# A hybrid streaming-encoder layer on one core: first rows taken by halves, a second plain feature tile, the down projection's first pieces split inside gate and up, attention's loads on another queue

## The chip, the cores and the metric

The kernel runs on one core of a Trainium2 chip. The metric is device time in microseconds (us) of one execution; the median of three runs is given. One further execution was taken by the hardware profiler, and all rows come from it.

## What is computed

One layer on x of 1024 rows (frames) by 1024 features, all float32:

```
x = x + 1/2 * swiglu(rms_norm(x), gate, up, down)       # FFN 1, d_ff = 2816
P = rms_norm(x) @ w_in                                   # 1024 x 3584
A = chunked band attention, 8 heads x 64, q and k RMS-normed, 9 chunks of 64 keys, relative bias
B = HGRN2 gated recurrence, 4 heads x 128, chunkwise, per-head RMS norm, swish gate
x = x + concat(A, B) @ w_out
x = x + 1/2 * swiglu(rms_norm(x), gate2, up2, down2)     # FFN 2
```

## The kernel before, in words

The instructions of each engine are written out by hand in program order; each engine is a strict queue, and semaphores order them against each other. There is no planner: where a line stands in its engine's list decides when it can run. Every matrix product is done three times in a reduced-precision float type (`three`, L636 to L638): high part times high part, high times low, low times high. So each operand is first split: ScalarE (ACT) copies it to its high part, VectorE (DVE) subtracts to get the low part.

**Stages, in order.** FFN 1: rows are normalised, transposed (features on partitions, `hThi`, `hTlo`) and multiplied. Gate and up go over 22 feature tiles of 128; each tile is 7 block products (Strassen-like, `gate_up`, which need sums t1, t2, t34 of the transposed rows, `hXhi`/`hXlo`, and sums of weights), only tile 0 is done plainly in 8 products (`plain`). A product is 12 matmuls of 128x512. The order at the start is the hand list `START` (15 products), the order in which weights are split is `WEIGHTS` (11, then 7 a tile), in a ring of 8 half places (`weight`). After product n both ACT and DVE prepare the weight that `PREPARED_AFTER` or `prepared_after` names, 7 products ahead. Down is 77 pieces (7 products x 11 pairs) in a ring of 4 (`piece_hi`, `piece_lo`, L1156 and L1568), of 12 matmuls each; its first piece is split when all 155 products are in. Then come the input projection (7 groups of 8 blocks, each of the last four with an HGRN head's matmuls hooked in), attention, the output projection in two column halves, and FFN 2 with the same code (F = 1).

**Start.** SyncE (SP) issues rows 0 to 3 of x (tiles of 128), gate and up of tile 0, rows 4 to 7, gate and up of tile 1. For each row tile ACT squares (L1047), GpSimd (POOL) takes the root (L1895, L1898), DVE normalises 1024 features (L1411), PE makes 8 transposes (L670), ACT copies the result back into `xs` (`keep_turned`, L1068) and from there to the high part (L1072), DVE makes the low part (L1425). The first product waits for four row tiles with all features. Product (1, 3) waits for `u2_ready`, which DVE gives at L1532 behind the weights of products to come.

**Attention.** Per pair of heads (4 pairs) there are 12 units; PE makes scores (L892), DVE adds the bias and takes the maximum (L1814), ACT exponentiates (L1335), PE turns (L905), DVE or ACT copies back (L1823, L1343), PE multiplies by values (L925). The first scores wait for `ro_ready`, the scaling of the last HGRN head's read-out (DVE L1763), whose banks they overwrite. POOL issues all loads: q and k (`load_qk`, L2036), bias (`load_bias`, L2040), v (`load_v`, L2044); it masks two corners of each bias tile after it has landed (`mask_bias`, L2052, L2053), scales q and k by their roots (`qk_rms`, L2060, L2063), and does the last head's gating (`finish`, L1998 to L2003) in between, all in one queue. Before exponentials of pair p come to an end ACT squares q and k of pair p + 1 (`square_qk`, L1285).

**Output projection.** SP issues w_out's pieces, then gate and up of FFN 2's tiles 0 and 1 (L501), then for each row tile the store of x (L620); the normalise of FFN 2 writes in place and waits for that store. PE turns tile t - 1 after row t of the second half. DVE's and ACT's first weights of FFN 2 come after all eight row tiles.

**End.** `take` (L1594) adds each of the last product's four banks once all 12 matmuls of the last piece are in; each is then stored.

Of the kernel before, what the change touches and what calls it, by code (L numbers as in the profile page):

```python
# [52 lines left out]

def slot(m):

    return (m + 1) % RING


def loads(m):
# [24 lines left out]

PLAIN_WEIGHT = (0, 1, 2, 3, 2, 3, 0, 1)
# [5 lines left out]
START = [(0, 0), (0, 1), (1, 0), (0, 2), (0, 3), (1, 2), (0, 4), (0, 5), (0, 6), (0, 7),  # L91
         (1, 4), (1, 1), (1, 3), (1, 5), (1, 6)]
PRODUCTS = START + [(e, i) for e in range(2, FT) for i in range(NPROD)]
WEIGHTS = [(0, 0), (0, 1), (1, 0), (0, 2), (0, 3), (1, 2), (1, 4), (1, 1), (1, 3), (1, 5), (1, 6)]\
    + [(e, i) for e in range(2, FT) for i in range(NPROD)]
# [5 lines left out]
PREPARED_AFTER = {8: [8], 9: [9, 10], 10: [11, 12], 11: [13], 12: [14, 15], 13: [16], 14: [17]}  # L101
# [6 lines left out]
def weight_no(e, i):  # L108
    return WEIGHTS.index((e, PLAIN_WEIGHT[i] if e == 0 else i))


def last_use(w):

    e, i = WEIGHTS[w]
    return seq(e, max(q for q in range(8) if PLAIN_WEIGHT[q] == i)) if e == 0 else seq(e, i)


def prepared_after(n):
    if n <= 14:
        return PREPARED_AFTER.get(n, [])  # L120
    return [n + 3] if n + 3 < NW else []
# [9 lines left out]
RAW_RING = 8  # L131
EVACS = NPROD * 4

# [50 lines left out]
def turn_bank(R, t):  # L184

    if R == R_FFN1:
        return (0, 2, 4, 6, 2, 6, 2, 6)[t]
# [4 lines left out]
    return 2 * (t % 2)  # L192

# [12 lines left out]
def build(nc, x, ffn1_norm_g, ffn1_w_gate, ffn1_w_up, ffn1_w_down, mix_norm_g, w_in, attn_q_norm_g,  # L206
# [3 lines left out]
    with ExitStack() as ctx:  # L210
# [50 lines left out]
        with ExitStack() as c:  # L261
            hThi = keep("hThi", [P, KT, T], F32R, c)
            hTlo = keep("hTlo", [P, KT, T], F32R, c)
            with ExitStack() as c2:
                hXhi = keep("hXhi", [P, 12, HALF], F32R, c2)
                hXlo = keep("hXlo", [P, 12, HALF], F32R, c2)
                gu_q = keep("gu_q", [P, HALF], where=c2)
# [40 lines left out]

        relrow = aT[0:AH, 0:N_REL]
# [6 lines left out]
        def weight(buf, w, F):  # L316

            at = (w + 2 * F) % PLACES
            return buf[:, at // 2, at % 2 * HALF:(at % 2 + 1) * HALF]

        def raw_weight(w):
# [3 lines left out]
            if e == 0:  # L325
# [38 lines left out]
        hT_ready = sem("hT_ready")  # L364
        z_copied = sem("z_copied")
# [70 lines left out]
        bias_loaded = sem("bias_loaded")  # L436
        bias_masked = sem("bias_masked")
# [31 lines left out]
        def score_bank(v):  # L469

            return 2 * ((v + 1) % 2)
# [6 lines left out]
        def _(sp):  # L478
            def piece(m, adv, src, shape):
# [5 lines left out]
                dst = raw[:, slot(m), :]  # L485
                if shape:
                    dst = dst.rearrange("p (k c) -> p k c", k=shape)
                sp.dma_start(dst, src).then_inc(raw_loaded[slot(m)], 16)

            def gate_up(F, e, w_gate, w_up):  # L490

                if e >= 2:
                    sp.wait_ge(w_ready, NW * F + (weight_no(e - 2, S4) if e > 2 else weight_no(0, 3)) + 1)
# [119 lines left out]
            for h in range(2):  # L613
# [1506 lines left out]
```

## Time and profile before

| | us |
|---|---|
| median of 3 runs (1974.49 to 1977.51) | 1974.71 |
| the profiled execution's own time | 1979.15 |
| its span, first to last instruction | 1977.6 |
| TensorE (PE) busy in it | 1897.7 |
| VectorE (DVE) busy | 1116.0 |
| ScalarE (ACT) busy | 676.9 |
| GpSimd (POOL) busy | 440.3 |

The profiled execution took 1.55 us more than its span, and 4.4 us more than the median. A view of the waits lists for each engine what ended its idle times; the chain of waits follows the last instruction back in time; the timeline gives each instruction with its start, its length and, in brackets, the idle time before it with its releaser. Matmul records overlap, so the pace of a row of matmuls is the distance of their starts. The granted TensorE clock is 1.00 at 2.4 GHz and about half in stretches at 1.2 GHz.

### The profile page before, as it was taken

To read this page: it belongs to the slowest core of one execution; us is meant where nothing else is said; L and a number is where in the kernel's file an instruction comes from. 1 tells how busy PE (TensorE), PEld (TensorE's weight loads), DVE (VectorE), ACT (ScalarE), POOL (GpSimd) and SP (SyncE) were. 2 spreads that over 40 slices of the span, in tenths; PEclk is the share of its full clock that TensorE was granted. 3 is DMA by queue.
4 is the path that set the end of the run, shared out by engine and by line. 5 is a ranking of instruction groups with operands and counts; after the bars stand their busy time and mean duration, and the time that the engine had idled before them with its cause. 6 is when DMAs were issued, how large, how long until landed. Compare 5 with 4: busy or idle time off the path is not lost.

```text
span 1977.6 us, 24542 instructions
## 1 busy us (share of the span) xinstructions
PE 1897.7 (96%) x9296; PEld 1570.5 (79%) x9296; DVE 1116.0 (56%) x1503; ACT 676.9 (34%) x1023; POOL 440.3 (22%) x350
## 2 busy tenths in 40 slices
PE   6899999999999999999998789989999999999998
PEld 5788888887888888888887567777888888878887
DVE  6866666665555630244545664348666666655564
ACT  7333333323333432211122563244333223323332
POOL 3322422431111100011223420001422422321030
PEclk9999999999999999999998999999999999999999
DMA  5454444537755343321342410114354444468663
GB/s 163 144 183 148 159 169 146 175 135 283 247 193 195 107 155 112 117 96 64 127 142 90 144 57 1 64 64 149 139 179 146 165 162 152 149 226 284 216 195 132
DMA packets 209004, 295.50 MB, mean 149 GB/s; under 512 B 14512, under 2 KB 104760, under 8 KB 208896
## 3 DMA queue, kind: packets, MB, share of 16 engines
q1 hardware_dynamic: 193184, 253.28, 37.5%
q0 software_dynamic: 7360, 25.51, 4.0%
q10 hardware_dynamic: 8352, 15.27, 2.1%
q8 instruction: 68, 1.11, 0.2%
q14 instruction: 40, 0.33, 0.1%
HBM read 205.37 MB, written 91.25 MB: 150 GB/s over the span
## 4 chain that ended last, share of the span: by engine, by line
PE 89%; DVE 5%; issue 2%; ACT 2%; DMA 1%; POOL 1%; DVEq 0%; SPq 0%; ACTq 0%; POOLq 0%
PE ps L636 27%; PE ps L638 27%; PE ps L637 27%; PE ps L809 2%; PE ps L670 1%; PE ps L905 1%; PE ps L892 1%; PE ps L925 1%; DVE wlo L1494 1%; DVE hXlo L1465 0%; DVE xs L1447 0%; DMA tok_scratch<-y 0%; DVE hTlo L1425 0%; DMA xs<-x 0%; PE ps L800 0%
## 5 line engine op out<-in xcount | busy, mean ns | idle before, releaser
L636 PE MATMUL ps<-hThi,whi 128*128 128x512 f32 x864 | 338.7, 392 | 11.9 <-DVE wlo L1494 6.4
L637 PE MATMUL ps<-hTlo,whi 128*128 128x512 f32 x864 | 337.6, 391 | 0.0
L638 PE MATMUL ps<-hThi,wlo 128*128 128x512 f32 x864 | 337.5, 391 | 0.0
L636 PE MATMUL ps<-whi 128*128 128x512 f32 x616 | 241.7, 392 | 9.2 <-DVE wlo L1568 9.2
L638 PE MATMUL ps<-whi,wlo 128*128 128x512 f32 x616 | 241.1, 391 | 0.0
L637 PE MATMUL ps<-wlo,whi 128*128 128x512 f32 x616 | 241.1, 391 | 0.0
L636 PE MATMUL ps<-hXhi,whi 128*128 128x512 f32 x504 | 197.9, 393 | 8.8 <-DVE wlo L1494 8.8
L636 PEld LDWEIGHTS ps<-hThi,whi 128*128 128x128 f32 x864 | 163.1, 189 | 46.0 <-DVE wlo L1494 6.6
L637 PE MATMUL ps<-hXlo,whi 128*128 128x512 f32 x504 | 197.3, 391 | 0.0
L638 PE MATMUL ps<-hXhi,wlo 128*128 128x512 f32 x504 | 197.3, 391 | 0.0
L638 PEld LDWEIGHTS ps<-hThi,wlo 128*128 128x128 f32 x864 | 163.0, 189 | 34.1
L637 PEld LDWEIGHTS ps<-hTlo,whi 128*128 128x128 f32 x864 | 163.2, 189 | 33.6
L1494 DVE TENSOR_TENSOR wlo<-raw,whi 128x512 fp32r<-128x512 f32 x176 | 128.4, 731 | 103.5 <-ACT whi L1103 103.5
L636 PE MATMUL ps<-whi,hThi 128*128 128x512 f32 x448 | 180.3, 403 | 1.1 <-DVE hTlo L1425 1.1
L638 PE MATMUL ps<-whi,hTlo 128*128 128x512 f32 x448 | 175.5, 392 | 0.0
L637 PE MATMUL ps<-wlo,hThi 128*128 128x512 f32 x448 | 174.7, 390 | 0.0
L1568 DVE TENSOR_TENSOR wlo<-raw,whi 128x1024 fp32r<-128x1024 f32 x80 | 113.6, 1426 | 83.1 <-ACT whi L1156 83.1
L1922 POOL TENSOR_TENSOR hidS<-hid 128x512 f32<-128x512 f32 x22 | 36.0, 1635 | 523.8 <-DVE hid L1562 523.8
L1103 ACT ACTIVATE whi<-raw 128x512 fp32r<-128x512 f32 x176 | 110.1, 627 | 123.3 <-PE ps L638 122.0
L636 PEld LDWEIGHTS ps<-whi 128*128 128x128 f32 x616 | 116.6, 189 | 34.3 <-DVE wlo L1568 10.0
L1568 DVE TENSOR_TENSOR wlo<-rawx,whi 128x1024 fp32r<-128x1024 f32 x74 | 93.9, 1269 | 81.4 <-ACT whi L1156 81.4
L638 PEld LDWEIGHTS ps<-whi,wlo 128*128 128x128 f32 x616 | 116.5, 189 | 24.5
(186 smaller groups left out, 2959.7 us busy)
## 6 DMA issues: line engine op xcount, KB each, us to landing
hid_scratch<-hid SPq DMA_DIRECT2D x132, 256.0 KB, 2.6
raw<-ffn_w_gate SPq DMA_DIRECT2D x44, 512.0 KB, 3.7
raw<-ffn_w_up SPq DMA_DIRECT2D x44, 512.0 KB, 4.9
wdb<-ffn_w_down SPq DMA_DIRECT2D x44, 512.0 KB, 4.1
wd_scratch<-wdb SPq DMA_DIRECT2D x88, 256.0 KB, 4.5
raw<-hid_scratch SPq DMA_DIRECT2D x80, 256.0 KB, 2.7
rawx<-hid_scratch SPq DMA_DIRECT2D x74, 256.0 KB, 2.7
raw<-w_in SPq DMA_DIRECT2D x28, 512.0 KB, 5.2
```

The lines of the kernel that those rows point to most:

```text
L636: pe.matmul(dst, ahi, bhi, start=first, stop=False, skip_group_check=onto)
L637: pe.matmul(dst, ahi, blo, start=False, stop=False, skip_group_check=onto)
L638: return pe.matmul(dst, alo, bhi, start=False, stop=last, skip_group_check=onto)
L670: mm = pe.transpose(ps[:, c0 + k * P:c0 + (k + 1) * P], src[:, k * P:(k + 1) * P], ident[:, :])
L809: mm = pe.matmul(ps[:, b * HALF + c * 64:b * HALF + (c + 1) * 64], hK[:, c * P:(c + 1) * P], q[:, c, :, 1, :], start=True, stop=True)
L892: last[hd] = pe.matmul(ps[:, b + c:b + c + m], qT[rows, p % 2, t * P:(t + 1) * P], kT[rows, p % 2, lo + c - c0:lo + c - c0 + m], start=Tru ...
L905: mm = pe.transpose(ps[:, 4 * HALF + c * P:4 * HALF + (c + 1) * P], Pr[:, v % SLOTS, c * P:(c + 1) * P], ident[:, :])
L925: mm = pe.matmul(ps[rows, b:b + P], vin[:, p % 2, t - n + 1 + c, rows], PT[:, (2 * w + hd) % SLOTS, c0 + c * P:c0 + (c + 1) * P], start=(c ...
L1103: act.activation(weight(whi, w, F), raw_weight(w), ACT.Copy).then_inc(w_hi_ready, 1)
L1494: dve.tensor_tensor(weight(wlo, w, F), raw_weight(w), weight(whi, w, F).bitcast(F32), ALU.subtract).then_inc(w_ready, 1)
L1568: dve.tensor_tensor(wlo[:, s, :], raw_piece(n), whi[:, s, :].bitcast(F32), ALU.subtract)\
L1922: pool.tensor_tensor(hidS[:, :], a11, a21, ALU.subtract).then_inc(hid_sums, 1)
```

## The change

In five places. **Start of FFN 1:** rows 0 to 3 are normalised, transposed and split by halves of 512 features (`early_norm`, `early_turn`, `early_hi_part`, `early_lo_part`; `early_keep` copies back afterwards from the bank), and the first product waits for the first halves alone; gate and up of tile 1 are loaded ahead of rows 4 to 7. **Both FFNs:** tile 1 is plain too (`NPLAIN` = 2, 8 products in place of 7, 156 in all), so the sums t1, t2, t34 are first needed at tile 2. **Down:** pieces 0 to 2 are split after products 1, 3 and 4 of the last tile; the ring places are shifted so that they fall in places that are free by then. **Attention:** SP issues the q, k, bias and v loads, bias and v of pairs 0 and 1 together, and the second half of w_out after them; the two masked corners are written once into the bias scratch in HBM by two DMAs of POOL; the first scores no longer wait for the read-out (head 1's go to banks 6 and 7), the read-out follows DVE's first two score passes. **Output projection and end:** gate and up of FFN 2 are issued after the stores of row tiles 2 and 4; FFN 2's first two weights are split before the last row tile; the last piece signals after each of its four banks.

```diff
+def raw_slot(m):
+    return (m + 1) % RING
 def slot(m):
-    return (m + 1) % RING
+    return (m + 3) % RING
...
+NPLAIN = 2
-START = [(0, 0), (0, 1), (1, 0), (0, 2), (0, 3), (1, 2), (0, 4), (0, 5), (0, 6), (0, 7),
-         (1, 4), (1, 1), (1, 3), (1, 5), (1, 6)]
+START = [(0, 0), (0, 1), (1, 0), (1, 1), (0, 2), (0, 3), (1, 2), (1, 3),
+         (0, 4), (0, 5), (1, 4), (1, 5), (0, 6), (0, 7), (1, 6), (1, 7)]
-PREPARED_AFTER = {8: [8], 9: [9, 10], 10: [11, 12], 11: [13], 12: [14, 15], 13: [16], 14: [17]}
+PREPARED_AFTER = {12: [8], 13: [9], 14: [10], 15: [11, 12], 16: [13, 14, 15]}
...
+PIECE_AFTER = [(FT - 1, 1), (FT - 1, 3), (FT - 1, 4)]
+def piece_slot(F, n):
+    return (n + 2 + 3 * F) % RING
+def early_bank(t):
+    return (2, 3, 6, 7)[t]
 def score_bank(v):
-            return 2 * ((v + 1) % 2)
+            return 6 if v == 1 else 2 * ((v + 1) % 2)
 # SyncE
             gate_up(0, 0, ffn1_w_gate, ffn1_w_up)
+            gate_up(0, 1, ffn1_w_gate, ffn1_w_up)
             for t in range(4, TT):
                 sp.dma_start(xs[:, t, :], x[0, t * P:(t + 1) * P, :]).then_inc(x_loaded[t], 16)
-            gate_up(0, 1, ffn1_w_gate, ffn1_w_up)
...
-            for e in range(2):
-                gate_up(1, e, ffn2_w_gate, ffn2_w_up)
+            out_pieces(0)
+            stored(6)
+            sp.wait_ge(y_ready, 2 * TT)
+            sp.wait_ge(turned, 2 * TT)
+            load_qk(0)
+            sp.wait_ge(bias_stored, 48)
+            sp.wait_ge(proj_done, PROJ_OUTS)
+            load_bias(0)
+            load_bias(1)
+            sp.wait_ge(qk_turned, 4)
+            load_qk(1)
+            stored(7)
+            load_v(0)
+            load_v(1)
+            out_pieces(1)
+            for p in range(2, PAIRS):
+                sp.wait_ge(qk_turned, 4 * p)
+                load_qk(p)
+                sp.wait_ge(unit_out, NU * (p - 1))
+                load_bias(p)
+                load_v(p)
             for t in range(TT):
                 sp.wait_ge(x_added, TT + t + 1)
                 sp.dma_start(x_d[t * P:(t + 1) * P, :], xs[:, t, :]).then_inc(x_saved[t], 16)
+                if t in (2, 4):
+                    gate_up(1, t // 2 - 1, ffn2_w_gate, ffn2_w_up)
 # TensorE
-                mm.then_inc(piece_done, 1)
+                    if t == 3 or F and n == NPIECE - 1:
+                        mm.then_inc(piece_done, 1)
...
             for t in range(4):
+                early_turn(t, 0)
+            products(0, 0, 1)
+            early_turn(0, 1)
+            early_turn(1, 1)
+            products(0, 1, 2)
+            early_turn(2, 1)
+            early_turn(3, 1)
+            for t in range(4, TT):
+                products(0, t - 2, t - 1)
                 turn_tile(R_FFN1, t)
+            products(0, 6, SEQ)
...
                 if w:
                     pe.wait_ge(unit_max, 2 * w)
                 else:
+                    pe.wait_ge(proj_evac, PROJ_OUTS)
+                if w == 1:
                     pe.wait_ge(ro_ready, HH + 1)
 # ScalarE, start
+            for t in range(3):
+                square(R_FFN1, t)
+            early_hi_part(0, 0)
+            square(R_FFN1, 3)
+            weight_hi(0, 0)
+            for t in range(1, 4):
+                early_hi_part(t, 0)
+            weight_hi(0, 1)
             for t in range(4):
+                early_keep(t, 0)
+            weight_hi(0, 2)
+            early_hi_part(0, 1)
+            early_hi_part(1, 1)
+            weight_hi(0, 3)
+            early_keep(0, 1)
+            early_keep(1, 1)
+            early_hi_part(2, 1)
+            early_hi_part(3, 1)
+            weight_hi(0, 4)
+            early_keep(2, 1)
+            early_keep(3, 1)
+            weight_hi(0, 5)
+            for t in range(4, TT):
                 square(R_FFN1, t)
 # ScalarE, last group of the projection: take_qk(0, 4) now ahead of the last split
+                    if q == 2 and square_at:
+                        act.wait_ge(proj_done, PROJ_OUTS)
+                        act.wait_ge(qk_gain_ready, 1)
+                        take_qk(0, 4)
 # ScalarE, FFN 2
-            for t in range(TT):
+            for t in range(TT - 1):
                 square(R_FFN2, t)
                 if t >= 2:
                     keep_turned(R_FFN2, t - 2)
+            weight_hi(1, 0)
+            weight_hi(1, 1)
+            square(R_FFN2, TT - 1)
+            keep_turned(R_FFN2, TT - 3)
 # ScalarE and VectorE, both FFNs (piece_hi on one, piece_lo on the other)
+                for n in range(12, SEQ):
+                    after_product(F, n)
+                    if PRODUCTS[n] in PIECE_AFTER:
+                        piece_hi(F, PIECE_AFTER.index(PRODUCTS[n]))
 # VectorE
+                if not prepare:
+                    read_out(j)
...
+            dve.wait_ge(bias_stored, 48)
...
+                if v == 1:
+                    read_out(HH - 1)
 # GpSimd
+            pool.memset(masked, MASKED).then_inc(mhalf_set, 1)
...
+            pool.dma_start(bias_d[:, CHUNK:P, 0:CHUNK].rearrange("h t s -> t h s"), corner)\
+                .then_inc(bias_stored, 16)
+            pool.dma_start(bias_d[:, 0:CHUNK, BAND - CHUNK:BAND].rearrange("h t s -> t h s"), corner)\
+                .then_inc(bias_stored, 16)
...
-            load_qk(0)
-            load_bias(0)
-            load_v(0)
-            mask_bias(0)
             finish(HH - 1)
             for p in range(1, PAIRS):
-                pool.wait_ge(qk_turned, 4 * p)
-                load_qk(p)
-                load_bias(p)
-                load_v(p)
-                mask_bias(p)
-                if p == 1:
+                if p == 2:
                     pool.wait_ge(ro_stored, 16 * HH)
```

## Rows read from the trace of the kernel before

**Rows 1.** The page: the span and the busy time of each engine.
```profile
span 1977.6 us, 24542 instructions
PE 1897.7 (96%) x9296; PEld 1570.5 (79%) x9296; DVE 1116.0 (56%) x1503; ACT 676.9 (34%) x1023; POOL 440.3 (22%) x350
```

**Rows 2.** Timeline, start of FFN 1, PE and DVE: start, length, what, [idle before].
```profile
14.48 1.29 DVE L1411 SCALAR_TENSOR_TENSOR xs<-xs,rstd,gain 128x1024 f32<-128x1024 f32 x1 [0.72 <-POOL rstd L1898]
22.40 0.77 PE L636 MATMUL ps<-hThi,whi 128*128 128x512 f32 x1 [5.48 <-issue]
27.62 1.91 PE L670 MATMUL ps<-ident,xs 128*128 128x128 f32 x16
...
67.77 0.77 PE L636 MATMUL ps<-hXhi,whi 128*128 128x512 f32 x1 [6.52 <-DVE wlo L1494]
```

**Rows 3.** Timeline of the same stretch, DVE further on.
```profile
45.75 2.49 DVE L1441 TENSOR_TENSOR xs<-xs 128x512 f32<-128x512 f32 x4
...
66.99 0.68 DVE L1532 TENSOR_TENSOR gu_u<-ps,gu_s 128x512 f32<-128x512 f32 x1
```

**Rows 4.** Chain of waits, start: one square of 128x1024 and its sum's read.
```profile
9.61 1.16 ACT junk L1047 x2
```

**Rows 5.** Timeline from gate and up to down, FFN 1: PE and SP's queue.
```profile
451.78 0.39 PE L638 MATMUL ps<-hThi,wlo 128*128 128x512 f32 x1
...
458.58 0.39 PE L638 MATMUL ps<-hThi,wlo 128*128 128x512 f32 x1
463.57 0.80 PE L636 MATMUL ps<-whi 128*128 128x512 f32 x1 [4.60 <-DVE wlo L1568]
...
467.96 0.39 PE L637 MATMUL ps<-wlo,whi 128*128 128x512 f32 x1
...
445.43 0.44 SPq L553 DMA_DIRECT2D raw<-ffn_w_down  x1
```

**Rows 6.** Timeline from projection to attention: ACT, PE, POOL.
```profile
1074.12 1.11 ACT L1302 ACTIVATE kT<-ps,qkg 128x1024 f32<-128x1024 f32 x1
...
1077.93 2.51 PE L892 MATMUL ps<-kT,qT 64*128 64x512 f32 x8 [4.89 <-DVE kS L1763]
1082.29 2.50 PE L892 MATMUL ps<-kT,qT 64*128 64x512 f32 x8 [1.85 <-DVE nmax L1814]
...
1094.71 1.33 PE L905 MATMUL ps<-ident,Pr 128*128 128x128 f32 x5 [5.74 <-ACT Pr L1335]
...
1087.10 0.89 POOL L2036 DMA_DIRECT2D y<-tok_scratch  x1
...
1092.79 1.06 ACT L1285 ACTIVATE junk<-y 128x1024 f32<-128x1024 f32 x1 [9.53 <-DMA y<-tok_scratch]
```

**Rows 7.** Timeline inside pair 1: POOL right after its masks, and PE.
```profile
1129.66 0.20 POOL L2060 TENSOR_SCALAR rsq<-ssq 128x16 f32<-128x16 f32 x1
...
1135.76 0.74 PE L905 MATMUL ps<-ident,Pr 128*128 128x128 f32 x5 [2.44 <-DVE PT L1823]
```

**Rows 8.** Timeline, output projection: SP's queue, DVE, PE.
```profile
1273.34 48.80 SPq L620 DMA_DIRECT2D x_scratch<-xs  x8
1279.38 1.28 DVE L1411 SCALAR_TENSOR_TENSOR xs<-xs,rstd,gain 128x1024 f32<-128x1024 f32 x1 [6.07 <-DMA x_scratch<-xs]
1280.72 1.97 PE L670 MATMUL ps<-ident,xs 128*128 128x128 f32 x8 [2.70 <-DVE xs L1411]
```

**Rows 9.** Timeline, FFN 2's first product and the end: PE and DVE.
```profile
1328.34 0.79 PE L636 MATMUL ps<-hThi,whi 128*128 128x512 f32 x1 [6.39 <-DVE wlo L1494]
1761.16 0.50 PE L636 MATMUL ps<-whi 128*128 128x512 f32 x1 [4.60 <-DVE wlo L1568]
1972.55 2.48 DVE L1594 SCALAR_TENSOR_TENSOR xs<-ps,xs 128x512 f32<-128x512 f32 x4 [8.50 <-PE ps L638]
```

**Rows 10.** DMA issues (KB each, us to landing), and the first head's start on DVE.
```profile
bias_scratch<-ext_scratch POOLq DMA_DIRECT2D x1, 2560.0 KB, 18.1
...
816.63 0.69 DVE L1716 TENSOR_SCALAR hK<-fF 128x1024 f32<-128x1024 f32 x1
```

More of the change, by code:

```diff
@@ L435, in build @@
         av_loaded = [sem(f"av_loaded{p}") for p in range(2)]
-        bias_loaded = sem("bias_loaded")
-        bias_masked = sem("bias_masked")
+        bias_loaded = [sem(f"bias_loaded{p}") for p in range(2)]
         qk_sq = sem("qk_sq")
@@ L1025, in split @@
             def split(m, adv=0):
-                s = slot(m)
-                act.wait_ge(raw_loaded[s], 16 * loads(m) + 4 * adv)
+                s, r = slot(m), raw_slot(m)
+                act.wait_ge(raw_loaded[r], 16 * loads(m) + 4 * adv)
                 if m < RING:
                     act.wait_ge(piece_done, NPIECE - 3 + m)
-                act.activation(whi[:, s, :], raw[:, s, :], ACT.Copy).then_inc(split_hi, 1)
+                act.activation(whi[:, s, :], raw[:, r, :], ACT.Copy).then_inc(split_hi, 1)
             def square(R, t):
@@ L1602, in down, with phases @@
                     take(F, q, 2 * (k - 2) + 1)
[L1604 to L1618 removed]
+            def phases(F):
+                for n in range(12, SEQ):
+                    after_product(F, n)
+                    if PRODUCTS[n] in PIECE_AFTER:
+                        piece_lo(F, PIECE_AFTER.index(PRODUCTS[n]))
+            for t in range(3):
+                early_norm(t, 0)
+            early_lo_part(0, 0)
+            early_norm(3, 0)
+            early_lo_part(1, 0)
+            weight_lo(0, 0)
+            early_lo_part(2, 0)
+            early_lo_part(3, 0)
+            weight_lo(0, 1)
+            for t in range(4):
+                early_norm(t, 1)
+            weight_lo(0, 2)
+            early_lo_part(0, 1)
+            early_lo_part(1, 1)
+            weight_lo(0, 3)
+            early_lo_part(2, 1)
+            early_lo_part(3, 1)
+            for t in range(4, TT):
+                weight_lo(0, t)
+                normalise(R_FFN1, t)
             for j in range(4):
@@ L1636, in _ @@
                 t34_lo(0, j)
-            for n in range(8, SEQ):
-                after_product(0, n)
+            phases(0)
             for n in range(NPIECE):
@@ L1854, in _ @@
                 normalise(R_FFN2, t)
-            t1_lo(1, 0)
-            for w in range(4):
+            for w in range(2, 6):
                 weight_lo(1, w)
@@ L1859, in _ @@
             t1(1, 2)
-            t1_lo(1, 1)
-            weight_lo(1, 4)
-            t1_lo(1, 2)
+            weight_lo(1, 6)
+            weight_lo(1, 7)
             hT_lo(R_FFN2, 7)
             t1(1, 3)
-            weight_lo(1, 5)
-            weight_sums(1, 1)
-            t1_lo(1, 3)
-            weight_lo(1, 6)
+            for j in range(4):
+                t1_lo(1, j)
             for j in range(4):
@@ L1877, in _ @@
                 t34_lo(1, j)
-            for n in range(8, SEQ):
-                after_product(1, n)
+            phases(1)
             for n in range(NPIECE):
```

417 lines of the change are left out of this document (210 added, 207 removed).

## The prediction

> **What bounds the kernel now.** I read the page first: of a span of 1977.6 us TensorE is busy 1897.7 [rows 1], so 80 us at most can be won by filling gaps, and every other engine counts only where TensorE waits for it. Then the waits of TensorE, and with the timeline the place of each. They lie in seven places: before the first product [rows 2], before product (1, 3) [rows 2], between gate-up and down of each FFN [rows 5, 9], where attention begins [rows 6], inside its pairs 1 and 2 [rows 7], at the first turn of the output projection [rows 8], before FFN 2's first product [rows 9]. Last comes the tail behind the last matmul [rows 9]. Each gap costs twice: the matmuls after it run at 1.2 GHz for a while. After the gap before down, ten steps from 463.57 to 467.96 take 4.39 us, where ten at full pace take 2.27: the 30 steps from 451.78 to 458.58 take 6.80, so 0.2267 a matmul and 2.72 us a product [rows 5]. A gap of 4.6 us thus gives back 2.1 more if it goes.
>
> **Down's first pieces.** The last product's next matmul would start at 458.81 and down starts at 463.57 [rows 5]: 4.76 of gap and 2.1 of slow matmuls. The change does these splits during the last tile, when no weights are left to split, on engines that are busy 34% and 56% of the span [rows 1]; raw pieces 0 to 3 were issued by 445.43, 13 us ahead [rows 5]. Cover: products 2 to 6 of that tile. **-6.9** in FFN 1. In FFN 2 the gap is the same 4.60 by its row [rows 9], the slow stretch I take 0.4 shorter: **-6.5**. Bounds: 4.6 (the clock stays as it is) and 6.9. What is late next is piece 4, loaded after the last product; it is needed four pieces, 10.9 us, later, and its load and splits take about 8 by the distance from issue to landing of other loads (5.7) [rows 6] and two splits of 1.2: just hidden, and the first thing to look at.
>
> **FFN 1's start.** Before, DVE begins to normalise row tile 3 at 14.48, and the first product runs at 22.40 [rows 2]. After, only 512 features are in front: 0.65 for the half normalise, 1.0 for 4 transposes (16 take 1.91 in a later row, at a partly slow clock), 0.6 each for the high and low half (four DVE halves take 2.49) [rows 3]; with 14.0 as start and the splits of weight 0 between, 17.0. That is 5.4 earlier. Against it: ACT now has six half copies or weight splits between the second early turns and the square of row tile 4. The first product ends at 22.4 (12 slow steps of 0.43), (0, 1) and the turns near 27.6; then 6 x 0.55, one square with its sum 1.16 [rows 4], POOL's root 0.9 (DVE waits 0.72 of it), the normalise 1.29 [rows 2]: row tile 4 is ready at 34.2. TensorE's turn of it stands behind (1, 0), which ends at 30.4: a new wait of 3.8, with 1.9 of slow matmuls after it. Sum to the end of tile 1's 16 products: 17.0 + 43.5 + 5.0 (48 transposes) + 2.7 (slow at first) + 3.8 + 1.9 = 73.9. The wait of 6.52 before 67.77 [rows 2] goes: t34 is needed for (2, 3) only. A smaller one comes there: DVE has 14 operations of 0.61 between the end of (1, 7) and the sum for (2, 3) (two weight splits, four for tile 1's hidden rows, two more splits, four weight sums, one split, the sum; before, it stood likewise behind weights, at 66.99) [rows 3]. With two short waits that is 9.3 against three products of 8.2: +1.1. Tile 2 begins in effect at 75.1. Before, the same 140 last products end at 458.81, so would have begun at 458.81 - 140 x 2.72 = 78.0. **-2.9**, in which the extra product's 2.7 is contained. Bounds: 0 (the waits grow by 3) and -6 (no wait at tile 4).
>
> **FFN 2's start.** The first product began at 1328.34, after 6.39 of waiting for a weight split that stood behind the last row tile [rows 9]. With two weights split before it, only row tile 5's copy remains in front, about 1324.9. Then 43.5 + 0.8 + 2.2 (slow) + 1.1 (the same DVE knot at (2, 3)) = 1372.5, against (1761.16 - 4.76) - 380.8 = 1375.6. **-3.1**; bounds 0 and -5.
>
> **Attention.** The k turn's copy ended at 1075.23; one copy of 1.0 is moved ahead of it, so 1074.2, and the first scores need no more than that: 3.7 before 1077.93 [rows 6]. The second scores wait for DVE: 2.0 for the first scores, two passes of 0.8 and the read-out of 1.2 give 1079.0, before 1082.29. From there to the turn at 1094.71 were 12.4, of which 5.74 were a wait for an exponential; ACT stood 9.53 for pair 1's q, issued at 1087.10 behind POOL's masks and gating and landed 5.7 later [rows 6]. SP can issue it at 1073, so it lands at 1078.8, in time. 1079.0 + 12.4 - 5.7 = 1085.7: 9.0 earlier, and 1.0 more for two rows of 8 score matmuls that ran slow at 2.5 (at the fast clock each would save 1.2). In pairs 1 and 2 POOL's root starts at 1129.66, right after masks that waited for a load; TensorE waited 2.44 at 1135.76 [rows 7], and as much in pair 2. Without the masks DVE is the next bound there, so I take half: 2.4 for both. **-12.4**; bounds -8 and -16. The price of moved work: SP's queue gets ten loads. Behind them stand w_out's second half, read only behind all of attention, and the x stores, the first at 1273.34 [rows 8]: covered. POOL gets two corner stores, DVE one more wait.
>
> **Output projection and tail.** The first x store was queued at 1273.34 behind 2 MB of weights; the normalise waited 6.07 for it, TensorE 2.70, and its turn ran slow (1.97 for 8) [rows 8]. With the store first it lands in time: 2.7 + 1.0 + 0.3 = **-4.0** (bounds -2.7, -4.3). The last four additions took 2.48 after the last matmul [rows 9]; three now run beside it: **-1.8** (-1.2, -2.0).
>
> **Sum.** -2.9 - 6.9 - 12.4 - 4.0 - 3.1 - 6.5 - 1.8 = -37.6. Against the profiled execution's own 1979.15 (1.55 over its span) that is 1941.6; it was 4.4 over the median of 1974.71, which gives 1937.1. The bounds sum to -21 and -46.
>
> **Weighed against a rule.** The rows of attention put the late loads down to their place in POOL's queue. The Trainium skill, "DMA: Bandwidth & Descriptors", section on issuing engines that are not separate DMA queues, says that all issuers share the same 16 engines, so a change of issuer saves only the issuing time, "usually small relative to the DMA itself". Where it alone holds, the first rival below comes true.
>
> **The rivals.** *The loads are no earlier.* The 1.3 MB of bias, 1 MB of q and k and 1 MB of v now start together at 1069 to 1076 and delay one another; ACT stands as long for q as before. Then the 9.0 shrinks to the first scores' 3.3 less what the loads cost, I take 1.4, and the pairs' 2.4 to 0: -26.6, 1948. For: a 5.7 us landing is already twice 512 KB's best. Against: w_out's 2 MB no longer lie in front. *Both starts come to nothing:* the turn of row tile 4 and the sum for (2, 3) cost 3 more each and TensorE falls to 1.2 GHz again: +6 to +11, 1946. *The pieces aren't ready:* piece 0's split on ACT waits behind its own load, or piece 4 is late, and both gaps stay: +13.4, 1950. *Slower:* the heads' DVE work now waits until both corner stores of POOL are in. The 2.5 MB before them took 18.1, so they start near 729, and the first head begins at 816.63 [rows 10]: 87 us of cover for 0.26 MB in 1024 pieces. It decides only past 87, and makes the kernel slower past 125; at 135 the time is 1947 + 38 = 1985. The nearest row speaks against it, by a factor of ten. That the change does not do what it says is the third rival: the splits would be in the right place in the list, and still late.
>
> **Chances.** Forecast 0.73 (by itself 1931 to 1944), loads 0.10, starts 0.08, pieces 0.06, slower 0.03. The range reaches from 1928 (near the sum of the lower bounds) to 1950, and so takes in the first three rivals. About 0.2% (4 us) is what a measurement of this kernel can tell from no change. Faster by more: 0.95; within: 0.02; slower: 0.03.
>
> **What would show it.** First product near 17, a wait of 3 to 4 at the turn of row tile 4, one of about 1 at (2, 3), in both FFNs; no gap before down and no slow matmuls there; second scores about 3 us after the read-out's sum, no exponential waiting for q; no wait at the output projection's first turn; one addition after the last matmul. Wrong I would be if new gaps over 3 us stood at piece 4 or in attention, since each also slows the matmuls after it, or if products ran at another pace than 2.72.

## The result, and the profile after

| | before | after |
|---|---|---|
| median of four runs each | 1975.99 (1974.49 to 1977.51) | 1954.07 (1953.03 to 1959.16) |
| profiled execution | 1979.15 | 1953.03 |
| its span | 1977.6 | 1951.5 |

The ratio of the times is 0.989, 95% interval 0.987 to 0.991: faster by 1.1%. The forecast was 1937.0 in a range of 1928 to 1950, so the direction held, and the time lies 4 us above the range. The spans differ by 26.1 us; 37.6 were forecast.

The page of the changed kernel, the two lines that answer to [rows 1]:

```profile
span 1951.5 us, 24554 instructions
PE 1894.9 (97%) x9320; PEld 1569.6 (80%) x9320; DVE 1104.8 (57%) x1491; ACT 674.8 (35%) x1027; POOL 420.4 (22%) x321
```

TensorE's idle time fell from 79.9 to 56.6, and with it 2.8 of busy time, although the second plain tiles add 24 matmuls: fewer ran at the slow clock (mean granted clock 0.984 before, 0.993 after). Where the forecast and the trace part is seen with the timeline, stage by stage, each row against the one of before. PE in FFN 1, start, length, what, [idle before it and its releaser], to be laid beside [rows 2, 5]:

```profile
17.33 0.77 PE L699 MATMUL ps<-hThi,whi 128*128 128x512 f32 x1 [2.26 <-DVE hTlo L1540]
33.49 1.97 PE L733 MATMUL ps<-ident,xs 128*128 128x128 f32 x8 [3.29 <-DVE xs L1522]
...
88.95 0.77 PE L699 MATMUL ps<-hXhi,whi 128*128 128x512 f32 x1 [6.53 <-DVE wlo L1625]
...
464.18 0.39 PE L701 MATMUL ps<-hThi,wlo 128*128 128x512 f32 x1
464.40 0.39 PE L699 MATMUL ps<-whi 128*128 128x512 f32 x1
```

The first two rows are the forecast's: first product at 17.0 (17.33), a wait of 3.8 at the turn of row tile 4 (3.29), and tile 2 begins at 74.05, where 73.9 was worked out. The last two rows show down's first matmul 0.22 behind the last product's last, which is the full pace, so its gap is gone. But at 88.95, before product (2, 3), TensorE waits 6.53 where the forecast has 1.1. The 13 matmuls behind it run slow and cost 2.7 more. Down therefore starts at 464.40, later than before (463.57), and gate and up are done 5.6 later than before (464.40 against 458.81), not 2.9 earlier: by itself the new start with the second plain tile made FFN 1 slower. With the slow stretch behind the old gap gone too, 1.3 us is all that FFN 1 gives: the recurrence's stage, at 822.52 before, comes at 821.21. 9.8 were forecast.

What VectorE does ahead of that product, and GpSimd beside it (timelines of the same stretch):

```profile
78.60 0.67 DVE L1650 TENSOR_TENSOR hid<-ps,gu_q 128x512 f32<-128x512 f32 x1
...
81.08 1.78 DVE L1625 TENSOR_TENSOR wlo<-sums,whi 128x512 fp32r<-128x512 f32 x1
82.78 1.75 DVE L1614 TENSOR_TENSOR sums<-raw 128x512 f32<-128x512 f32 x1
84.45 1.74 DVE L1615 TENSOR_TENSOR raw<-raw 128x512 f32<-128x512 f32 x1
86.23 0.69 DVE L1617 TENSOR_TENSOR sums<-raw 128x512 f32<-128x512 f32 x1
...
88.17 0.68 DVE L1672 TENSOR_TENSOR gu_u<-ps,gu_s 128x512 f32<-128x512 f32 x1
```

```profile
78.71 1.30 POOL L2064 TENSOR_TENSOR wdb<-wdb 128x512 f32<-128x512 f32 x1
80.64 1.68 POOL L2074 TENSOR_TENSOR hidS<-hid 128x512 f32<-128x512 f32 x1 [0.63 <-DVE hid L1653]
82.39 1.59 POOL L2076 TENSOR_TENSOR hid<-hid 128x512 f32<-128x512 f32 x1
84.06 1.59 POOL L2079 TENSOR_TENSOR hid<-hid 128x512 f32<-128x512 f32 x1
```

To be seen: VectorE has no idle time here. TensorE goes on 0.10 after the end of the sum at L1672, the last of the list (88.85); the row of TensorE names the split before it as the releaser, but in experiment 1, where the sum stands ahead of that split, TensorE does not wait for either. A VectorE operation whose two inputs both lie in SBUF lasts 1.74 to 1.78 while GpSimd goes from one sum to the next, one for each of GpSimd's; as soon as GpSimd stops (85.65) the same form takes 0.69. One that meets only part of a sum is stretched less, or not at all (1.18 at 79.38; 0.68 at 80.48, begun before GpSimd's sum at 80.64). The one that reads PSUM (`ps`, 78.60) takes 0.67 although GpSimd works then too, up to 78.63 and again from 78.71. The Trainium skill, "GPSIMD Engine Reference", section Key points, says that GpSimd shares its SBUF interfaces with VectorE and contends with VectorE's instructions with two SBUF inputs. By that rule these rows stretch and the PSUM row does not; the trace agrees, and gives the size, 2.6 times.

The trace of before had such rows as well, one of them ahead of the sum of [rows 3], and the forecast passed over them:

```profile
65.21 1.31 POOL L1906 TENSOR_TENSOR wdb<-wdb 128x512 f32<-128x512 f32 x1 [31.80 <-DMA wdb<-ffn_w_down]
```

```profile
65.32 1.75 DVE L1494 TENSOR_TENSOR wlo<-sums,whi 128x512 fp32r<-128x512 f32 x1
```

There it stretched one operation ahead of that sum (and one of 1.52 in each later pair of tiles, where TensorE did not wait for it). In the changed kernel the sum comes 21 us later, behind the hidden-row operations of tiles 0 and 1: GpSimd's four sums of down's weights (73.83 to 80.01) and three of the sums that the hidden rows release (from 80.64) all fall ahead of it.

Attention, PE, ACT and SP's queue, to be laid beside [rows 6, 7]:

```profile
1077.41 2.20 PE L975 MATMUL ps<-kT,qT 64*128 64x512 f32 x8 [2.97 <-DVE kS L1914]
...
1083.83 0.77 PE L988 MATMUL ps<-ident,Pr 128*128 128x128 f32 x5
...
1123.31 0.74 PE L988 MATMUL ps<-ident,Pr 128*128 128x128 f32 x5 [1.52 <-DVE PT L1977]
...
1193.82 1.31 PE L1006 MATMUL ps<-PT,v_in 128*64 128x128 f32 x20
```

```profile
1077.06 1.05 ACT L1400 ACTIVATE junk<-y 128x1024 f32<-128x1024 f32 x1
```

```profile
1071.76 0.37 SPq L647 DMA_DIRECT2D y<-tok_scratch  x1
```

The turn that stood 5.74 for an exponential now comes at 1083.83 without a wait, 10.9 earlier than 1094.71; the waits inside pairs are 1.5 instead of 2.4. ScalarE squares q of pair 1 at 1077.06 without standing for it. From 1065 to the output projection the stage is 15.3 shorter (12.4 forecast). Of that, 1.6 lies in its last stretch alone, between the same two waits of 1.0 and 0.84, where in the trace of before 20 matmuls ran slow that take 1.31 at 1193.82:

```profile
1209.04 2.40 PE L925 MATMUL ps<-PT,v_in 128*64 128x128 f32 x20
```

This is the granted clock of one execution and not the change: in the runs of experiments 5 and 8, whose attention is the changed kernel's, such a row of 20 is slow again (2.36 and 2.30).

Output projection, FFN 2 and the end, PE and DVE, beside [rows 8, 9]:

```profile
1261.28 1.03 PE L733 MATMUL ps<-ident,xs 128*128 128x128 f32 x8
...
1303.82 0.77 PE L699 MATMUL ps<-hThi,whi 128*128 128x512 f32 x1 [2.85 <-ACT xs L1165]
...
1364.33 0.63 PE L699 MATMUL ps<-hXhi,whi 128*128 128x512 f32 x1 [4.85 <-DVE wlo L1625]
...
1738.66 0.39 PE L699 MATMUL ps<-whi 128*128 128x512 f32 x1
```

```profile
1946.26 2.73 DVE L1733 SCALAR_TENSOR_TENSOR xs<-ps,xs 128x512 f32<-128x512 f32 x4 [6.46 <-PE ps L701]
```

The first turn runs at the full pace without a wait; the first product comes 24.5 earlier than 1328.34, so this stage gave 7.9. Then the wait at (2, 3) is there again, 4.85. From the first product to down it takes 434.8, where the forecast has 428.4: down starts 22.5 earlier than before (1738.66 against 1761.16), although its own gap of 4.6 is gone, so FFN 2's gate and up became 6.8 longer. (Before, they had a wait of 2.25 at product (1, 3), which the forecast's list of gaps leaves out; it is contained in its 1375.6.) At the end VectorE's four additions begin before the last matmul (1947.88).

### The profile page after: what moved, and what is told of

Its sections match the earlier page's. It is cut to its first block, busy times and chain, and to the rows that moved or that the text cites. A ratio compares the mean times of both kernels' runs of the same rounds, so it can differ in the third digit from the quotient of the medians.

```text
span 1951.5 us, 24554 instructions
## 1 busy us (share of the span) xinstructions
PE 1894.9 (97%) x9320; PEld 1569.6 (80%) x9320; DVE 1104.8 (57%) x1491; ACT 674.8 (35%) x1027; POOL 420.4 (22%) x321
## 4 chain that ended last, share of the span: by engine, by line
PE 93%; DVE 3%; issue 2%; ACT 2%; DMA 1%; SPq 0%; POOL 0%; ACTq 0%; DVEq 0%
PE ps L699 28%; PE ps L701 28%; PE ps L700 28%; PE ps L890 2%; PE ps L988 1%; PE ps L975 1%; PE ps L733 1%; PE ps L1006 1%; DMA raw<-ffn_w_up 1%; DVE wlo L1625 0%; DVE S L1966 0%; PE ps L911 0%; ACT PT L1455 0%; PE ps L881 0%; PE ps L914 0%
## 5 line engine op out<-in xcount | busy, mean ns | idle before, releaser
L699 PE MATMUL ps<-hThi,whi 128*128 128x512 f32 x896 | 352.6, 394 | 5.1 <-ACT xs L1165 2.8
L700 PE MATMUL ps<-hTlo,whi 128*128 128x512 f32 x896 | 351.0, 392 | 0.0
L701 PE MATMUL ps<-hThi,wlo 128*128 128x512 f32 x896 | 350.8, 392 | 0.0
L699 PEld LDWEIGHTS ps<-hThi,whi 128*128 128x128 f32 x896 | 169.8, 190 | 41.0 <-issue 5.7
L699 PE MATMUL ps<-hXhi,whi 128*128 128x512 f32 x480 | 188.5, 393 | 11.4 <-DVE wlo L1625 11.4
L701 PEld LDWEIGHTS ps<-hThi,wlo 128*128 128x128 f32 x896 | 169.7, 189 | 35.5
L700 PEld LDWEIGHTS ps<-hTlo,whi 128*128 128x128 f32 x896 | 169.9, 190 | 35.0
L700 PE MATMUL ps<-hXlo,whi 128*128 128x512 f32 x480 | 188.4, 392 | 0.0
L701 PE MATMUL ps<-hXhi,wlo 128*128 128x512 f32 x480 | 188.2, 392 | 0.0
L1707 DVE TENSOR_TENSOR wlo<-raw,whi 128x1024 fp32r<-128x1024 f32 x80 | 106.4, 1329 | 78.7 <-ACT whi L1252 78.4
```

Source lines behind the costliest of these rows:

```text
L699: pe.matmul(dst, ahi, bhi, start=first, stop=False, skip_group_check=onto)
L700: pe.matmul(dst, ahi, blo, start=False, stop=False, skip_group_check=onto)
L701: return pe.matmul(dst, alo, bhi, start=False, stop=last, skip_group_check=onto)
L1707: dve.tensor_tensor(wlo[:, s, :], raw_piece(n), whi[:, s, :].bitcast(F32), ALU.subtract)\
```

## The experiments

Two questions. What makes the wait at (2, 3): the order of VectorE's list, GpSimd's work beside it, or something of TensorE's own? And did the terms that came out right come out so for the reasons given? Times are medians against runs of the kernel before on the same chip; the changed kernel's ratio, 0.989, is the mark. The intervals of the ratios reach 2.4 to 4.3 us to either side, so by time alone two versions less than that apart are not told from each other.

**1. The sum ahead of the weights.** VectorE makes the sum for (2, 3) ahead of two weight splits and four weight sums that stood before it (ScalarE's list follows).

```
-PREPARED_AFTER = {..., 15: [11, 12], 16: [13, 14, 15]}
+PREPARED_AFTER = {..., 15: [11, 12], 16: [13], 17: [14, 15], 18: [16, 17]}
```

> The u2 operation of (2, 2) is put ahead of two weight splits and of weight sums in VectorE's order. Theory (what stands before the sum of (2, 3) in VectorE's queue is what TensorE waits for): the wait of 6.53 in FFN 1 and that of 4.9 in FFN 2 shrink below 1 us each, and the slow matmuls behind them go with them, about 2 each; span 12 to 15 us shorter, time about 1940. Rival (weights of tile 2 are late by their own load, or an extra product was miscounted): the waits only move to the next weight, the time stays within 3 us of 1954.

Measured: 1944.64, ratio 0.9831 (0.9817 to 0.9844). Both waits at (2, 3) are gone, so the weights' loads and the count of products are not what TensorE waited for. In FFN 2 nothing over 0.8 comes in its place; in FFN 1 a new wait stands 6 us later, before (2, 6) (PE, DVE, and SP's queue):

```profile
95.28 0.77 PE L699 MATMUL ps<-hThi,whi 128*128 128x512 f32 x1 [5.19 <-DVE hid L1658]
```

```profile
94.44 0.69 DVE L1658 TENSOR_TENSOR hid<-ps,gu_u 128x512 f32<-128x512 f32 x1 [4.17 <-DMA hid_scratch<-hid]
```

```profile
84.42 0.43 SPq L524 DMA_DIRECT2D raw<-ffn_w_gate  x1
84.90 0.58 SPq L524 DMA_DIRECT2D raw<-ffn_w_up  x1
85.53 3.70 SPq L545 DMA_DIRECT2D hid_scratch<-hid  x2
```

VectorE may not overwrite the hidden rows until they are stored, and their store is queued behind tile 4's weights. In the changed kernel this wait was hidden under the 6.53. So two thirds of what was expected came: 9.4 of 14.

**2. GpSimd's sums held back.** VectorE's list is the changed kernel's; GpSimd alone waits.

```
+                pool.wait_ge(u2_ready, (FT - NPLAIN) * F + 1)
                 for k in range(NPAIR):
                     down_sums(F, k)
                     hid_pair_sums(F, k)
```

> GpSimd's sums of down's weights and of hidden rows begin only after the u2 operation of tile 2; VectorE's order is as in the changed kernel. Contention theory: VectorE's operations with two inputs in SBUF (weight splits' low halves, weight sums) last 0.7 in front of (2, 3) instead of 1.7 to 1.8, the wait of 6.53 falls to 1 to 2 us in FFN 1, and in FFN 2, 4.9 to about 1.5; time 5 to 11 us lower, unless GpSimd's work is now late for a later product (a new wait at (2, 6) or at tile 3). Queue theory (count of operations alone): the durations and waits stay as they are, 6.5 and 4.9, time within 2 us of 1954.

Measured: 1971.56, ratio 0.9966 (0.9954 to 0.9978): 17.5 slower than the changed kernel, and yet the clearest answer. VectorE and PE:

```profile
79.30 0.68 DVE L1625 TENSOR_TENSOR wlo<-sums,whi 128x512 fp32r<-128x512 f32 x1
79.90 0.69 DVE L1614 TENSOR_TENSOR sums<-raw 128x512 f32<-128x512 f32 x1
...
83.16 0.68 DVE L1672 TENSOR_TENSOR gu_u<-ps,gu_s 128x512 f32<-128x512 f32 x1
```

```profile
83.94 0.47 PE L699 MATMUL ps<-hXhi,whi 128*128 128x512 f32 x1 [1.60 <-DVE wlo L1625]
107.47 0.77 PE L699 MATMUL ps<-hThi,whi 128*128 128x512 f32 x1 [15.12 <-DVE hid L1658]
```

The same operations in the same order now last 0.68 each, and the wait at (2, 3) is 1.60 in FFN 1 and 1.60 in FFN 2. So 4.93 of the 6.53 is contention, and what remains is near the 1.1 of the forecast's count. The price is the one named beforehand: GpSimd's sums and their stores are late for (2, 6), 15.12 in FFN 1 and 14.29 in FFN 2.

**3 and 4. The turn of row tile 4 one product later**, alone and with the first edit.

```
-            for t in range(4, TT):
-                products(0, t - 2, t - 1)
+            products(0, 2, 4)
+            turn_tile(R_FFN1, 4)
+            for t in range(5, TT):
+                products(0, t - 1, t)
                 turn_tile(R_FFN1, t)
```

> TensorE takes the turn of row tile 4 one product later, with product (1, 1) ahead of it. Theory (row tile 4 is ready at 36.8 whatever TensorE does before): the wait of 3.3 at that turn falls to about 0.6, and 2.7 us less is lost there; but the knot at (2, 3) is set by VectorE, so its wait grows by nearly as much, 6.5 to 8 or 9, and the time stays within 2 us of 1954. Rival (the waits are independent): 2.5 to 4 us lower, 1950 to 1951.

> Both edits. If the knot at (2, 3) hid the gain of the later turn, both together are 2 to 4 us faster than the u2 order alone: about 1937. If the next turns (row tiles 5 to 7) are the bound, no faster than it: about 1940.

Measured: 1952.19 (0.9871, 0.9856 to 0.9885) and 1945.5 (0.9837, 0.9824 to 0.9849). The wait of 3.29 falls to 0.56. Most of it comes back at once in two other waits, 1.19 for ScalarE (35.18) and 1.35 for the hidden rows (73.86); the rest comes back at the knots, as 6.89 for 6.53 at (2, 3) and, with the first edit, as 5.93 for 5.19 at (2, 6). The knots stand at nearly the same time as without the turn's edit (89.19 against 88.95, 96.35 against 95.28). So nothing is gained at them by what TensorE does earlier; both times lie within the noise of the kernels that they start from. Neither 1937 nor 1940 came for the fourth: the expectation left out the second knot, which had not been seen yet.

**5. Hidden rows stored first.** With the first edit; SyncE stores tile 1's hidden rows and two of the sums ahead of `load_down(1)` and tile 4's weights, in both FFNs.

```
+                    if e == 2:
+                        store_hid_sum(F, 0, S3)
+                        store_hid_sum(F, 0, S1)
                     if e + 2 < FT:
                         gate_up(F, e + 2, w_gate, w_up)
...
                         store_down_sums(F, e // 2)
+                        if e == 1:
+                            store_hid(F, 1, A12)
+                            store_hid(F, 1, A22)
```

> As a1_u2_first, and SyncE puts the stores of tile 1's hidden rows and of the pair's first two sums ahead of the loads of down's next pair and of tile 4's weights. Theory (the 5.19 that TensorE waits at 95.28 in a1_u2_first is VectorE waiting for a hidden buffer whose store stands behind those loads in SyncE's queue): the stores land 4 to 5 us earlier, the wait falls below 1, and with the slow matmuls behind it 5 to 8 us go: 1937 to 1940. Rival (the store itself, or GpSimd's sums before it, is the bound): the wait keeps 3 us or more, time above 1942.

Measured: 1945.96 (0.9843, 0.9827 to 0.9859), no better than the first. In FFN 1 the wait fell from 5.19 to 2.39, in the theory's direction but not below 1. FFN 2 got one of 4.38 that was not there, which the expectation had not thought of:

```profile
1368.63 0.77 PE L708 MATMUL ps<-hThi,whi 128*128 128x512 f32 x1 [4.38 <-DVE hid L1667]
```

```profile
1361.54 1.78 DVE L1634 TENSOR_TENSOR wlo<-raw,whi 128x512 fp32r<-128x512 f32 x1
1363.25 1.77 DVE L1634 TENSOR_TENSOR wlo<-sums,whi 128x512 fp32r<-128x512 f32 x1
1364.94 1.75 DVE L1634 TENSOR_TENSOR wlo<-raw,whi 128x512 fp32r<-128x512 f32 x1
```

```profile
1357.74 1.62 POOL L2091 TENSOR_TENSOR hid<-hid 128x512 f32<-128x512 f32 x1
1359.33 1.74 POOL L2067 TENSOR_TENSOR wdb<-wdb 128x512 f32<-128x512 f32 x1
```

The earlier store let GpSimd go on at once (in the first experiment it stood 3.25 for the store at this place), and three splits that took 0.69 there take 1.77 here. The wait for a store had been keeping GpSimd out of VectorE's way.

**6. With the later turn, and row tile 5's copy in FFN 2 ahead of the last square on ScalarE.**

```
             weight_hi(1, 1)
-            square(R_FFN2, TT - 1)
             keep_turned(R_FFN2, TT - 3)
+            square(R_FFN2, TT - 1)
```

> As b1_u2_stores, with the later turn of row tile 4 of a3_turn_later, and with row tile 5's copy in FFN 2 ahead of the last square on ScalarE. With nothing behind it that absorbs the gain, the later turn is worth 1 to 3 us, and the copy brings FFN 2's first product forward by 1.7 (its wait of 2.85 falls to 1.2): 1933 to 1937. If another wait takes each gain, it stays at b1_u2_stores.

Measured: 1942.46 (0.9826, 0.9812 to 0.984), 3.5 below 5, where 9 to 13 were expected: a miss. FFN 2's first product no longer waits for that copy; both knots stand (2.84 and 4.38).

**7. The stores moved in FFN 1 only.** The lines of 5 with `F == 0 and` in front.

> As b2_all, with the stores moved ahead in FFN 1 only. Theory (the 4.38 of b1_u2_stores and b2_all in FFN 2 came from the earlier stores there: they let GpSimd go straight on with the next four sums, beside which VectorE's weight splits last 1.7 to 1.8): in FFN 2 the splits after the weight sums are at 0.7 again and the wait is gone, as in a1_u2_first; with the slow matmuls behind it 5 to 7 us: 1936 to 1938. Rival (FFN 2's wait came from ScalarE's or TensorE's other order): it stays at 4 us, time 1942.

Measured: 1935.97 (1934.89 to 1936.29), ratio 0.9793 (0.9779 to 0.9806). FFN 2's wait is gone, and the splits there are short again:

```profile
1352.88 0.68 DVE L1636 TENSOR_TENSOR wlo<-raw,whi 128x512 fp32r<-128x512 f32 x1
1353.48 0.68 DVE L1636 TENSOR_TENSOR wlo<-sums,whi 128x512 fp32r<-128x512 f32 x1
1354.08 0.68 DVE L1636 TENSOR_TENSOR wlo<-raw,whi 128x512 fp32r<-128x512 f32 x1
```

This is the fastest version, about 18 us under the changed kernel and 2.1% under the one before.

**8. GpSimd's sums of hidden rows ahead of its first sums of down's weights, FFN 1.**

```
+                if F == 0:
+                    hid_pair_sums(0, 0)
+                    down_sums(0, 0)
-                for k in range(NPAIR):
+                for k in range(1 - F, NPAIR):
```

> As b3_stores_ffn1, and in FFN 1 GpSimd makes the first pair's sums of hidden rows ahead of its first sums of down's weights. If GpSimd's work is only moved beside VectorE's operations of a later product, the wait of 2.8 before product (2, 6) is the same or larger, and the time within 2 us of b3_stores_ffn1. If it matters that VectorE's two splits before tile 1's hidden rows aren't stretched and the sums start 1 us earlier, the wait falls under 1.5 and 1 to 3 us go: 1934 to 1936.

SyncE's stores and loads of that pair follow the new order, so down's next pair is loaded later too.

Measured: 1939.68 (0.9814, 0.98 to 0.9827), 3.7 slower than 7. The operations before tile 1's hidden rows are short, as hoped, but GpSimd's eight sums now run on end to 91.3, and the splits behind the weight sums are stretched instead. A miss: the contention is not less, it is elsewhere, and the wait grew from 2.94 to 4.07. One more of 1.68 comes at 109.96, behind GpSimd's next four sums, which the later load has put beside VectorE's list there.

**9 and 10. Place or issuer.** q and k of pair 1 issued late by SyncE; and all q and k issued by GpSimd, but at the places in time that SyncE has.

```
             sp.wait_ge(qk_turned, 4)
-            load_qk(1)
             stored(7)
             load_v(0)
             load_v(1)
             out_pieces(1)
+            load_qk(1)
```

> SyncE issues pair 1's q and k behind v and behind w_out's second half, at about 1079.5 instead of 1071.8; all else is the changed kernel. Place theory (what mattered is where the load stands in a queue, whoever issues it): q lands 8 to 12 us later, ScalarE stands for it at 1077 as GpSimd's late issue made it stand before, and TensorE's second turn of exponentials waits again: 5 to 12 us slower than the changed kernel, 1960 to 1966. Rival (the gain came from the other issuer, or from the masks that GpSimd lost): within 2 us of 1954.

> GpSimd issues all q and k loads, at the same places in time as SyncE does in the changed kernel (behind the same waits, early). Place theory: q of pair 1 is issued near 1072 to 1073, lands before or just after 1077, and the time is within 1.5 us of the changed kernel's 1954. Issuer theory (GpSimd's queue is slower, or its sums are held up by issuing): the loads land 3 us or more later, and waits of 2 us and more return in attention; 1957 or above.

Measured: 1959.69 (0.9914, 0.9892 to 0.9935) and 1953.26 (0.9883, 0.9862 to 0.9903). The late load from the quick queue brings ScalarE's and TensorE's waits back; the early load from GpSimd's queue costs nothing. ACT and PE of the first, then POOL and ACT of the second:

```profile
1087.94 1.06 ACT L1400 ACTIVATE junk<-y 128x1024 f32<-128x1024 f32 x1 [13.30 <-DMA y<-tok_scratch]
```

```profile
1089.86 1.33 PE L988 MATMUL ps<-ident,Pr 128*128 128x128 f32 x5 [6.89 <-ACT Pr L1447]
```

```profile
1072.17 0.95 POOL L2201 DMA_DIRECT2D y<-tok_scratch  x1 [16.41 <-PE ps L935]
```

```profile
1077.93 1.06 ACT L1396 ACTIVATE junk<-y 128x1024 f32<-128x1024 f32 x1 [0.65 <-DMA y<-tok_scratch]
```

GpSimd's issue takes 0.95 instead of 0.37, and from the start of the issue to the landing it is 5.7 instead of 5.3: the load is there 0.65 after ScalarE asks for it. In 9 the load is issued at 1076.64, and it also takes 11.3 to land, beside the 2 MB of w_out that SyncE issued just before it. From the first scores to the output projection attention lasts 128.3 in the changed kernel, 137.5 in 9 and 128.2 in 10; the profiled execution of 9 gets 2.5 back in FFN 1, where fewer matmuls ran slow. On the same chip all runs of 9 lie above all runs of 10, by 6.4 in the medians.

The rule of the Trainium skill weighed in the prediction, that another issuer saves only its issuing time, agrees with 10, and yet the rival that the prediction tied to it did not come true: the gain came from the place in the queue, 15 us earlier than GpSimd's issue at 1087.10 in [rows 6]. Bias and v on SyncE and the masks in HBM stay in both runs, so their share was not tried by itself.

**11. The x stores behind the weights again.**

```
+            for e in range(2):
+                gate_up(1, e, ffn2_w_gate, ffn2_w_up)
             for t in range(TT):
                 sp.wait_ge(x_added, TT + t + 1)
                 sp.dma_start(x_d[t * P:(t + 1) * P, :], xs[:, t, :]).then_inc(x_saved[t], 16)
-                if t in (2, 4):
-                    gate_up(1, t // 2 - 1, ffn2_w_gate, ffn2_w_up)
```

> Only the order of SyncE's issues is put back in the output projection: both weight tiles of FFN 2 ahead of all x stores. If the term of 4.0 was right, the normalise waits about 6 us for the store's landing again, TensorE 2.7 at the first turn, that turn runs slow (1.97 for 8), and FFN 2's first product comes 3.5 to 4 us later; profiled time 1957. If another wait hides it, under 1.5.

One execution, 1955.57, span 1954.0 (2.5 above the changed kernel's). DVE and PE:

```profile
1262.71 1.28 DVE L1522 SCALAR_TENSOR_TENSOR xs<-xs,rstd,gain 128x1024 f32<-128x1024 f32 x1 [6.08 <-DMA x_scratch<-xs]
```

```profile
1264.06 1.09 PE L733 MATMUL ps<-ident,xs 128*128 128x128 f32 x8 [2.71 <-DVE xs L1522]
```

Both waits are back within 0.01 (6.07 and 2.70 in [rows 8]), and every later turn is 2.8 to 2.9 later. But the turn runs at 1.09, not at 1.97 as in [rows 8]: here a stop of 2.71 did not bring the slow clock. Up to FFN 2's first product 2.9 of the term of 4.0 is shown by this one execution. The rest was the slow stretch: from this turn to the next there are 7.79 in the trace of before, 6.40 here.

**12. Down's first pieces split behind the last tile again**, the loads left where they are.

```
-PIECE_AFTER = [(FT - 1, 1), (FT - 1, 3), (FT - 1, 4)]
+PIECE_AFTER = []
```

> Only the splits of down's first three pieces go back behind the last tile; the loads of pieces stay where they are. If the term of 6.9 and 6.5 was right, TensorE waits some 4.6 us before down in both FFNs, and the matmuls behind run slow for about 2.1: 13 us slower, 1967. Rival (the wait before down came from the loads, or from the slots of pieces, not from the place of the splits): the gap stays closed or half of it, under 1960.

Measured: 1967.68 (1960.89 to 1968.14; 0.994, 0.9919 to 0.996), 13.6 above the changed kernel by the medians, where 13.4 were worked out; by the means it is 10.7, because two of the five runs took 1960.9 and 1964.1. PE, both FFNs:

```profile
469.06 0.80 PE L699 MATMUL ps<-whi 128*128 128x512 f32 x1 [4.60 <-DVE wlo L1707]
...
1751.43 0.80 PE L699 MATMUL ps<-whi 128*128 128x512 f32 x1 [4.59 <-DVE wlo L1707]
```

Both gaps are back in full, 4.76 each from where the next matmul would have started, and the slow matmuls behind them cost 1.7 and 2.2: 13.4 in the trace. The rival, loads or places in the ring, is refuted.

## Why the prediction was right in its direction and wrong in its size

The forecast missed by 17.1 us (1954.07 against 1937.0). 11.5 of that lies between the terms' 37.6 and the spans' 26.1. The rest, 5.6 with the rounding, lies in the step from the profiled execution to the median: the forecast took off 4.4, because the profiled run of before stood that far over the median of three. The profiled run of after stands 1.0 under its own. A profiled run that stands above the median shows the scatter of runs, not a fixed cost; the 4.4 should have gone into the range and not into the number. In the later sets of 8 to 11 runs before's median was 1976.6 to 1978.2, and single runs went from 1973.6 to 1982.1.

The 11.5 by stages: FFN 1 gave 8.5 less than forecast, FFN 2 from its first product to down 6.4 less, attention 2.9 more, the output projection with FFN 2's first product 0.5 more, down and the tail what was forecast.

Point by point:

- **Down's first pieces, -13.4 in sum: right.** No gap in either FFN, piece 4 in time, and the undoing costs 13.6 by the medians (10.7 by the means).
- **FFN 1's start: the step that failed** is "with two short waits that is 9.3 against three products of 8.2: +1.1". Everything before it stands within about 0.5 us. The count of 14 operations was right; their price of 0.61 was not. Four of them, with two SBUF inputs and beside GpSimd's sums, took 1.74 to 1.78 each, two more 0.86 and 1.18. The wait was 6.53 for 1.1, and 2.7 for slow matmuls behind it, which the sum does not have. Without GpSimd beside them the same list gives 1.60 (experiment 2). The start with its second plain tile cost 5.6 where -2.9 was forecast; with down's 6.9 FFN 1 gave 1.3 of 9.8.
- **FFN 2's start: failed by the same step**, "the same DVE knot at (2, 3)": 4.85 for 1.1, with 1.7 for slow matmuls behind it, and 3.0 instead of 2.2 for those behind the first product. The first product's own part came as worked out: 7.9 for it and the output projection together against 7.4.
- **The rival "both starts come to nothing"** had the place and what follows, but put 3 us more on the turn of row tile 4, which came as forecast, and 3 on the sum for (2, 3), and held it for 0.08. Measured were 5.4 and 3.8 more at (2, 3). The row of 1.75 beside GpSimd's 1.31 in the trace of before was the price it needed; four such operations in a list of 14, each 1.1 longer, give 4.4 of the 5.4 that were missing, and the two stretched in part 0.7 more.
- **Attention, -12.4 forecast, 15.3 measured: right in mechanism.** Up to the turn at 1083.83, 9.6 came, where 10.0 were worked out (9.0 and 1.0 of clock). The rest was undersized: from there to the output projection 5.7, not 2.4. One period of a pair (between the turns of k) fell from 33.06 and 31.49 to 30.53, so 3.5 for the two pairs. Of the remaining 2.2, 1.6 is the slow row at 1209.04 in the trace of before, luck of the clock, and 0.7 lies right behind the turn at 1094.71, where the matmuls of before run slow. Without the luck the stage gave 13.7. The rival "the loads are no earlier" is refuted by the trace (no wait for q at 1077.06); 9 and 10 show that the early issue did it, not the issuer.
- **Output projection, -4.0:** 2.9 of it is shown by the undoing, in one execution; the rest was the slow stretch of [rows 8], no fixed companion of the wait.
- **Tail, -1.8:** 1.9 by the spans' ends.
- **"Slower" by the corner stores:** nothing of it in the trace; the recurrence's stage starts 1.3 earlier than before.
- **Weighed against a rule:** the rule of the Trainium skill held and the first rival did not (experiment 10), so the two were not one.

So the forecast's 1937 was within reach of this design: version 7, which changes only the order of lists, takes 1935.97.

## What to carry to other kernels

When operations are counted to see whether a list fits its time, price each at the duration that it has beside what the other engines will do then. Look for the longest row of the form, not only the mean, and see what GpSimd did at that moment. After a wait is removed, the next one is often at hand, hidden under it; and a wait of an engine off the path can be what keeps it out of the way of one that is on it. Free the path's engine by the order of its own list first: what must come out first stands first.

## What the runs showed of the hardware

- A VectorE operation of 128x512 float32 with two SBUF inputs takes 0.68 alone (experiment 2) and 1.74 to 1.78 in a row of them beside GpSimd's sums of the same size; they go one for one. One that meets part of a sum takes less (0.86, 1.18). GpSimd's sum suffers less: 1.26 to 1.30 alone (experiment 2, at 90.33 to 93.06), mostly 1.6 to 1.7 beside. VectorE operations that read one input from PSUM stay at 0.68. The size was not expected: a pair of one each takes 1.70, where one after the other would take 2.0, so running side by side saves only 0.3.
- GpSimd's issue of a load takes 0.95, SyncE's 0.37; from the start of the issue to the landing it was 5.7 and 5.3 for the same load at the same place. The same load issued behind 2 MB took 11.3 (experiment 9).
- A stop of TensorE of 2.71 was followed by a turn of 1.97 in one kernel and by one of 1.09 in another, at the same place in the code. With the code ahead of it the same as well, the stop of 3.29 before the turn of row tile 4 was followed by 1.97 in the changed kernel and by 1.09 in the profiled execution of experiment 9:

```profile
32.34 1.09 PE L733 MATMUL ps<-ident,xs 128*128 128x128 f32 x8 [3.28 <-DVE xs L1522]
```
